# Weighted sums of expert rows in a decoder step: 64x64 tiles of the array in place of 128x128

## The reference

```python
sc, sel = lax.top_k(cand, P_TOPK)
eidx = jnp.take_along_axis(cidx, sel, axis=-1)
g = jax.nn.softmax(sc, axis=-1)
act = jax.nn.gelu(jnp.einsum('td,thkd->thk', xb, u[eidx]))
return jnp.einsum('thk,thkd->td', (g * act), v[eidx])
...
x = x + g2 * peer(n2, ...)
```

## Time and profile before

| | before |
|---|---|
| median of 3 runs | 5520.86 us (5513.3 to 5524.6) |
| the profiled execution | 5515.14 us |
| its span, first to last instruction | 5513.0 us |
| PE busy | 4234.7 us, 77% |
| DVE busy | 2665.5 us, 48% |
| POOL busy | 1701.3 us, 31% |
| ACT busy | 1041.0 us, 19% |
| bytes moved by DMA | 1431.24 MB |

### The profile page before, as it was taken

How to read it: one execution, slowest core, us unless ns; L and a number is a source line. 1 busy time by engine, 2 the same in 40 slices (tenths; PEclk the granted TensorE clock), 3 DMA queues, 4 the chain that set the end, 5 groups by cost and what they waited for, 6 DMA issues and landing times. The chain is left out here.

```text
span 5513.0 us, 49784 instructions
## 1 busy us (share of the span) xinstructions
PE 4234.7 (77%) x14045; PEld 2514.6 (46%) x14045; DVE 2665.5 (48%) x6121; ACT 1041.0 (19%) x2778; POOL 1701.3 (31%) x1436
## 2 busy tenths in 40 slices
PE   6499999999535667939967877778777777777777
PEld 1387766778434563528833333333333333333332
DVE  1201222110346321231157777777776777777775
ACT  0102122110432100010012222222222222222221
POOL 0231221222015300001134444444444444444442
PEclk8699888889757558959878898988889888888888
DMA  6222222122356624131179999999999999999998
GB/s 212 78 82 69 65 77 66 61 75 71 143 200 232 231 97 172 43 100 41 53 290 421 421 421 421 421 421 421 421 421 421 421 421 421 421 421 421 421 421 345
DMA packets 340769, 1431.24 MB, mean 260 GB/s; under 512 B 41214, under 2 KB 105886, under 8 KB 203395
## 3 DMA queue, kind: packets, MB, share of 16 engines
q0 software_dynamic: 165744, 1156.98, 51.3%
q1 hardware_dynamic: 151940, 229.27, 12.3%
q10 hardware_dynamic: 23000, 43.91, 2.1%
HBM read 1345.38 MB, written 91.87 MB: 261 GB/s over the span
## 5 line engine op out<-in xcount | busy, mean ns | idle before, releaser
L1954 PE MATMUL peer_acc<-uv_ring,diag 128*128 128x512 f32 (+1 forms) x4224 | 2002.4, 635 | 629.0 <-ACT diag L1916 624.7
L1776 POOL DMA_INDIRECT uv_ring<-in_peer_uv,idx_all x1056 | 1204.6, 1141 | 1550.3 <-PE peer_acc L1954 1344.7
L1954 PEld LDWEIGHTS peer_acc<-uv_ring,diag 128*128 128x128 f32 (+1 forms) x4224 | 838.0, 202 | 1798.5 <-issue 1629.5
L1845 DVE SCALAR_TENSOR_TENSOR uv_ring<-uv_ring,n_rows 128x1024 f32<-128x1024 f32 x1056 | 1263.6, 1224 | 582.9 <-DMA uv_ring<-in_peer_uv,idx_all 548.0
L1916 ACT ACTIVATE diag<-ident,weight_all 128x128 f32<-128x128 f32 x1024 | 327.3, 390 | 152.4 <-DVE weight_all L1857 144.0
L1912 ACT ACTIVATE gelu_now<-act_now 128x4 f32<-128x4 f32 x264 | 54.2, 205 | 1541.5 <-DVE uv_ring L1845 1533.3
L729 PE MATMUL h_acc<-in_w_lo,n_hi 128*128 128x512 f32 x720 | 317.3, 441 | 0.0
L729 PE MATMUL h_acc<-in_w_hi,n_lo 128*128 128x512 f32 x720 | 308.4, 428 | 0.0
L729 PE MATMUL h_acc<-in_w_hi,n_hi 128*128 128x512 f32 x720 | 304.9, 424 | 0.0
L725 PE MATMUL h_acc<-n_hi,in_w_lo 128*128 128x512 f32 (+1 forms) x672 | 244.1, 363 | 38.1 <-POOLq L449 38.1
L520 ACT COPY h_stage<-h_acc 128x512 f32<-128x512 f32 x174 | 89.5, 519 | 964.0 <-PE h_acc L729 544.2
(11 more groups left out here) (287 smaller groups left out, 5129.6 us busy)
## 6 DMA issues: line engine op xcount, KB each, us to landing
in_w<-in_w_in POOLq DMA_DIRECT2D x68, 512.0 KB
ada_w<-in_w_ada SPq DMA_DIRECT2D x12, 2048.0 KB
q_broadcast<-qk_rows_dram SPq DMA_DIRECT2D x24, 1024.0 KB
h_r<-h_stage SPq DMA_DIRECT2D x80, 256.0 KB
uv_ring<-in_peer_uv,idx_all POOLq DMA_INDIRECT x1056, 26.4
past_keys<-in_cache_kv_g SPq DMA_DIRECT2D x16, 1024.0 KB
h_t<-h_stage SPq DMA_DIRECT2D x56, 256.0 KB
qk_raw<-h_r SPq DMA_DIRECT2D x8, 1536.0 KB, 8.6
```

The lines of the kernel that those rows point to most:

```text
L1776: nc.gpsimd.indirect_dma_start(uv_ring[:, k % SLOTS_UV, :], None, x["peer_uv"][0], bass.IndirectOffsetOnAxis(ap=idx_all[:, g * TOPK + k:g ...
L1845: nc.vector.scalar_tensor_tensor(out=uv_ring[:, k % SLOTS_UV, 0:D], in0=uv_ring[:, k % SLOTS_UV, 0:D], scalar=1.0, in1=n2_rows[:, :], op0= ...
L1954: ins = nc.tensor.matmul(acc[0:w, c, :], diag[:, k % RING, 0:w], uv_ring[:, k % SLOTS_UV, D + c * 512:D + (c + 1) * 512], start=False, sto ...
```

## The change

For the prompt tiles each expert's matmuls are cut into 64x64 tiles of the array. The first 64 tokens (`r` = 0) use array rows 0 to 63, the last 64 (`r` = 1) rows 64 to 127. The columns, and with them the PSUM partitions that get the result, are `(r + k) % 2 * 64`: for even `k` the same half as the rows, for odd `k` the other. Each `r` has PSUM banks of its own, so `peer_acc` grows to [128, 2, 2, 512]. `diag` shrinks to 64 columns; its pattern `halves` is the identity's left half plus its right half. The two partial sums of each token (even and odd experts) are added when the tile ends: ACT copies all four banks to `half_sums`, and PE multiplies with `halves` into `folded` (`add_halves`, four matmuls 128x64), which DVE reads in the residual. The ninth tile keeps its 128x32 matmuls and passes through the same fold. The zero matmuls that open and close a tile become four each. PE's loops over tiles and steps are now Python loops, so its program is straight code.

```diff
-    diag = sb("diag", [P, RING, P])
+    diag = sb("diag", [P, RING, HALF])
+    halves = sb("halves", [P, HALF])
-    acc = psum("peer_acc", [P, 2, 512])
+    acc = psum("peer_acc", [P, 2, 2, 512])
+    folded = psum("peer_folded", [P, 2, 512])
...
+        nc.vector.tensor_tensor(halves[:], ident[:, 0:HALF], ident[:, HALF:P], ALU.add).then_inc(fold_ready, 1)
...
-            dve.wait_ge(sum_copied, t + 1)
-            link(nc.vector.tensor_tensor(moe_sum[0:w, :], moe_sum[0:w, :], gate[0:w, :], ALU.mult))
+            dve.wait_ge(halves_added, t + 1)
+            link(nc.vector.tensor_tensor(moe_sum[0:w, :], folded[0:w].rearrange("p a b -> p (a b)"), gate[0:w, :], ALU.mult))
...
-                act.wait_ge(y_ready, t)
-            nc.scalar.activation(moe_sum[0:w, :], acc[0:w].rearrange("p a b -> p (a b)"), ACT.Copy).then_inc(sum_copied, 1)
+                act.wait_ge(halves_added, t)
+            nc.scalar.activation(half_sums[:], acc[:], ACT.Copy).then_inc(sum_copied, 1)
...
-            with pe.Fori(first, end) as g:
+            for g in range(first, end):
                 for k in range(TOPK):
                     pe.wait_ge(diag_ready, g * TOPK + (k + 1))
                     pe.wait_ge(uv_landed[k % SLOTS_UV], g * 16 + 16)
-                    for c in range(2):
-                        ins = nc.tensor.matmul(acc[0:w, c, :], diag[:, k % RING, 0:w], uv_ring[:, k % SLOTS_UV, D + c * 512:D + (c + 1) * 512],
-                                               start=False, stop=False)
+                    if g < S_FIRST:
+                        for c in range(2):
+                            for r in range(2):
+                                rows, to = slice(r * HALF, r * HALF + HALF), (r + k) % 2 * HALF
+                                ins = nc.tensor.matmul(acc[to:to + HALF, r, c, :], diag[rows, k % RING, :],
+                                                       uv_ring[rows, k % SLOTS_UV, D + c * 512:D + (c + 1) * 512], start=False, stop=False)
...
                     ins.then_inc(v_free, 1)
...
+        def add_halves(t):
+
+            pe.wait_ge(sum_copied, t + 1)
+            pe.wait_ge(fold_ready, 1)
+            if t:
+                pe.wait_ge(y_ready, t)
+            for r in range(2):
+                for c in range(2):
+                    ins = nc.tensor.matmul(folded[r * HALF:(r + 1) * HALF, c, :], halves[:], half_sums[:, r, c, :],
+                                           start=True, stop=True)
+            ins.then_inc(halves_added, 1)
+
+        for t in range(N_TILES):
+            tile(t, t * PH, t * PH + PH if t < N_TILES - 1 else N_STEPS)
+            if t < N_TILES - 1:
+                add_halves(t)
+        add_halves(N_TILES - 1)
```

More of the change, by code:

```diff
@@ L1647, in peer_phase @@
     FOLD = P // S_TOK
+    HALF = P // 2
     S_FIRST = (N_TILES - 1) * PH
@@ L1679, in peer_phase @@
     x1_rows = sb("x1_rows", [P, D])
+    half_sums = sb("half_sums", [P, 2, 2, 512])
     moe_sum = sb("moe_sum", [P, D])
@@ L1701, in peer_phase @@
     sum_copied = sem("sum_copied")
+    halves_added = sem("halves_added")
     n2_loaded = sem("n2_loaded")
@@ L1921, in copy_sum @@
             if not (isinstance(t, int) and t == 0):
-                act.wait_ge(y_ready, t)
-            nc.scalar.activation(moe_sum[0:w, :], acc[0:w].rearrange("p a b -> p (a b)"), ACT.Copy).then_inc(sum_copied, 1)
+                act.wait_ge(halves_added, t)
+            nc.scalar.activation(half_sums[:], acc[:], ACT.Copy).then_inc(sum_copied, 1)
         exps(0)
-        steps(0, PH, ident, True)
+        act.wait_ge(fold_ready, 1)
+        steps(0, PH, halves, True)
         copy_sum(0, P)
         with act.Fori(1, N_TILES - 1) as t:
-            steps(t * PH, t * PH + PH, ident, True)
+            steps(t * PH, t * PH + PH, halves, True)
             copy_sum(t, P)
-        act.wait_ge(fold_ready, 1)
+        act.wait_ge(fold_ready, 2)
         steps(S_FIRST, N_STEPS - 1, fold, True)
@@ L1938, in _, with tile @@
         pe.wait_ge(consts_ready, 3)
[L1940 to L1945, removed]
+        def tile(t, first, end):
+            if t:
                 pe.wait_ge(sum_copied, t)
+            for r in range(2):
                 for c in range(2):
-                    nc.tensor.matmul(acc[:, c, :], zeros[:, 0:P], zeros[:, :], start=True, stop=False)
-            with pe.Fori(first, end) as g:
+                    ins = nc.tensor.matmul(acc[:, r, c, :], zeros[:, 0:P], zeros[:, :], start=True, stop=False)
+            if t == 0:
+                ins.then_inc(v_free, SLOTS_UV)
+            for g in range(first, end):
                 for k in range(TOPK):
@@ L1952, in tile @@
                     pe.wait_ge(uv_landed[k % SLOTS_UV], g * 16 + 16)
-                    for c in range(2):
-                        ins = nc.tensor.matmul(acc[0:w, c, :], diag[:, k % RING, 0:w], uv_ring[:, k % SLOTS_UV, D + c * 512:D + (c + 1) * 512],
-                                               start=False, stop=False)
+                    if g < S_FIRST:
[4 more added lines that the diff above has]
+                                                       uv_ring[rows, k % SLOTS_UV, D + c * 512:D + (c + 1) * 512], start=False, stop=False)
+                    else:
+                        rows = slice(0, P)
+                        for c in range(2):
+                            ins = nc.tensor.matmul(acc[0:S_TOK, 0, c, :], diag[:, k % RING, 0:S_TOK],
+                                                   uv_ring[rows, k % SLOTS_UV, D + c * 512:D + (c + 1) * 512], start=False, stop=False)
@@ L1956, in tile @@
                     ins.then_inc(v_free, 1)
-            for c in range(2):
-                ins = nc.tensor.matmul(acc[:, c, :], zeros[:, 0:P], zeros[:, :], start=False, stop=True)
+            for r in range(2):
+                for c in range(2):
+                    ins = nc.tensor.matmul(acc[:, r, c, :], zeros[:, 0:P], zeros[:, :], start=False, stop=True)
             ins.then_inc(sum_ready, 1)
-        tile(0, 0, PH, P)
-        with pe.Fori(1, N_TILES - 1) as t:
-            tile(t, t * PH, t * PH + PH, P)
@@ L1965, in _ @@
-        tile(N_TILES - 1, S_FIRST, N_STEPS, S_TOK)
+        def add_halves(t):
+            pe.wait_ge(sum_copied, t + 1)
+            pe.wait_ge(fold_ready, 1)
+            if t:
+                pe.wait_ge(y_ready, t)
+            for r in range(2):
+                for c in range(2):
+                    ins = nc.tensor.matmul(folded[r * HALF:(r + 1) * HALF, c, :], halves[:], half_sums[:, r, c, :],
+                                           start=True, stop=True)
+            ins.then_inc(halves_added, 1)
```

## The result

The changed kernel takes **5529.72 us** (median; 5519.7 to 5546.33), the kernel before, run on the same chip in turns with it, 5516.39 us (5513.3 to 5524.6). The ratio is **1.0024, 95% interval 1.0015 to 1.0033**: slower by 0.24%, 13 us. The profiled execution took 5525.42 us with a span of 5523.9 us; of before it was 5515.14 and 5513.0.

What follows compares the result with a forecast made beforehand. Gather DMA was taken to bound the expert stage: 5515.1 + 0 (matmuls) + 0 (boundaries) + 6.1 (tail) + 5.6 (code) = 5526.8 us, or 5532.6 on the median's footing. Forecast 5533 us, range 5517 to 5585.

Steps and rivals of the forecast that it cites:

- What bounds: Expert stage: the DMA queue of expert-row gathers sets the pace, share 1.01 at 421 GB/s, 2.51 us an expert.
- PE's work: Expert matmuls in the stage: 0.86 to 1.71 us an expert, under the DMA's 2.51 us, so worth 0.
- Rival 3: Expert matmuls: tiles run singly, PE needs 3.43 us an expert, stage grows 940 us to about 6465 us; chance 0.05.
- Tile boundaries: The 8 tile ends: PE late by 1 to 8 us, covered by 18 us of queued DMA work, so 0.
- Code: PE's straight code in the expert stage: 71 fetches of 16 KB on the full DMA, +5.6 us.
- even spread: PE's code fetches fall evenly on all 16 DMA engines: 89/16 = 5.6 us; likeliest case, chance 0.50.
- bounds of two engines or one: PE's code fetches in the stage: 45 us if on two DMA engines, 89 us if on one.
- Rival 1: PE's code fetches fall on few DMA engines: 5572 us on two, 5616 us on one; chance 0.28.
- Rival 2: Expert stage: code fetches stay hidden and only the tail counts, 5527 us, within 0.2%; chance 0.10.
- Tail: After the last expert: more zero records, a larger copy and the fold, without cover, +6.1 us (5 to 10).
- Gathers take longer from issue to landing: Sign in the expert stage: gathers' time from issue to landing rises from 26.3 us.
- POOL waiting less for PE: Sign in the expert stage: POOL, which issues the gathers, waits less for PE; no size given.

Runs made afterwards that it cites:

- e1: The changed kernel with PE's tiles and steps back in loops on the chip, as in the kernel before; ratio to before 1.0004.
- e9: The changed kernel with PE in loops, only u halves gathered, and even and odd experts kept to the columns of their own row half; 4762.51 us.
- e8: The changed kernel with PE in loops, gathering only the u half of each row, dots over 512 columns; 4566.88 us.
- e3: The changed kernel with 17 more instructions on PE for each prompt expert, waits that are always met; ratio to before 1.0049.
- e10: The kernel before with POOL's gathers in a loop over pairs of steps instead of straight code; ratio to before 0.9995.
- e12: The kernel before with more always-met waits on POOL ahead of every gather, thus more POOL code to fetch; ratio to before 1.0084.
- e7: The changed kernel, PE's code straight, gathering only the u half of each row, dots over 512 columns; 4561.86 us.
- e2: The kernel before with PE's loops written out as straight code, nothing else changed; ratio to before 1.0002.
- e11: The changed kernel with POOL's gathers in a loop over pairs of steps, PE's code still straight; ratio to before 1.0028.
- half-row kernels: The kernel before and the changed kernel, each gathering only the u half of each row, dots over 512 columns; 4730.06 and 4561.86 us.

## Why the prediction was right, and where its terms were not

The forecast was 5533 us, 0.21% over before, and the result is 0.24% over (1.0015 to 1.0033). Its mechanism holds: matmuls worth nothing, code and tail the whole cost. The sum was 11.7 us and the two traces differ in stage and tail by 12.0; but two terms missed in opposite directions, the code by 3.4 us and the tail by 3.1. That the total is so close is luck.

- **What bounds.** Right: DMA share 1.01 and 421 GB/s on both sides, steps of 40.17 us.
- **PE's work, 0 in the stage.** Right, by e1's stage (0.1 us). The range of 0.86 to 1.71 us for an expert was right: 3.89 us for four is 0.97 us each with the first one's filling in it. Rival 3 (singly running tiles) is out. Tiles in different rows and columns run together here, by the 3.89 us against 7.15 us, and e9 against e8 shows the condition: four do not when consecutive experts stay in the same column halves (1.83 us an expert against 1.62, with PE busy for 396 of 400 us against 326).
- **Tile boundaries, 0.** Right, by e1 again. At the boundary of the earlier trace rows the order of things was as foreseen, with the end of the residual, the fold, the zeros and POOL's gather:

```profile
4124.09 1.22 DVE L1883 TENSOR_TENSOR x_rows<-x_rows,moe_sum 128x1024 f32<-128x1024 f32 x1
...
4125.46 2.85 PE L1985 MATMUL peer_folded<-half_sums,halves 128*64 128x512 f32 x8 [3.58 <-DVE x_rows L1883]
4128.24 4.44 PE L1953 MATMUL peer_acc<-zeros 128*128 128x512 f32 x8
...
4132.61 2.86 PE L1964 MATMUL peer_acc<-uv_ring,diag 64*64 64x512 f32 x24
...
4135.33 0.94 POOL L1781 DMA_INDIRECT uv_ring<-in_peer_uv,idx_all  x1 [13.73 <-PE peer_acc L1964]
```

  From the end of the residual (4125.31 us) PE takes 7.3 us to the first expert, where before took 5.9: 1.4 us more, at the low end of the 1 to 8 foreseen. POOL's gather comes 10.0 us after the residual, where before had 10.4 (4120.83 to 4131.27), so it is not late at all. The 4 us between 4131.27 and 4135.33 lie ahead of this boundary: the residual itself ends 4.5 us later, by the time the stage had lost so far.
- **Code, +5.6 foreseen, +9.0 measured.** This term was mis-sized, and its mechanism was half right. The right half: the fetches take time of the DMA engines that the gathers fill (0.2% of the 16 engines' time for the 67 on queue 8 in after's table, and 22.5 us more of stage for 137 fetches in e3), and the last of 16 parts sets a gather's landing. The number of fetches was right (71 foreseen, 69 more measured). The step that failed is the even spread: I had the fetch near 3170 us, which delayed nothing, and read it as spreading over all 16 engines. It said only that the part it moved was not the latest one. Eight parts are late in after, not 16, and a fetch puts one back by 1.5 us, not 1.26. That makes 69 x 1.5 / 8 = 12.9 us, less the lead that POOL's late part gave to all others (2.7 us by e10, 3.3 by the landings): about 10 us for 9.0 measured. The packet of a fetch itself takes 1.07 us in after's records (median of 67) and one of POOL's 0.31 us; why they put one part back by 1.5 and 0.70 us is not shown. The bounds of two engines or one were too far out for PE. Rival 1's reason for them, that a processor's fetches always go to one engine, fits POOL's (in e12 one part is 15.3 us late, and 67 fetches cost 46.6 us) and not PE's (eight parts late).
- **Rival 2, the code hidden.** Out: the stage grew by 9.0 us for 69 fetches and by 22.5 for 137. Where the DMA has room nothing contradicts it, but e8 against e7 could not show 9 us.
- **Tail, +6.1 foreseen, +3.0 in this pair.** The four zeros came out right (1.93 to 3.65 us, +1.7) and so did the copy (1.02 to 1.89 us, +0.9 for 0.7). The fold took 1.98 us, under the range of 2.6 to 7 and under the 3.4 us of eight records in a row, so some of them overlap; presumably that is because its halves, too, go to different column halves. And the 16 records of the sample tile, which the change does not touch, took 7.05 us after and 8.66 before, because the granted clock was 1.00 in the one and 0.81 in the other. In e2, e10 and e12, whose tails are before's, they take 7.05 us and the tail 17.9 us; so at the same clock the tail grew by 22.5 - 17.9 = 4.6 us, 1.5 under the forecast, and the fold is the term that was too large. In e11, at a granted clock of 0.70, they take 10.01 us, the fold 3.15 at 0.56, and the tail 26.7.
- **Gathers take longer from issue to landing.** The row says the opposite: a median of 21.6 us after, 26.3 before. But that view takes its median from few gathers: 61 of before, all of slot 8 of the ring, and 123 of after, of slots 0 and 9, and the time to landing depends on the slot (19.5 us for slot 0 and 30.2 for slot 15 in before). Over all gathers of the stretch whose 16 records of completion are in the trace (868 and 966) the median goes from 25.9 to 27.4 us. Pairing the n-th issue with the n-th dot (gathers 100 to 950) gives a mean of 29.4 us after and 28.5 before. So it came true, and is small.
- The rest of what I said would show it held: PE's busy time is down by a third, and queue 8 has about 70 fetches. **POOL waiting less for PE** did not come true. From 2900 to 5400 us it waits as long as before. The waits (engine, line, waited for: us in total, times, longest) are, in after and then in before:

```profile
POOL uv_ring L1781 <- PE peer_acc L1964: 1275.3, 302, 16.8
```

```profile
POOL uv_ring L1776 <- PE peer_acc L1954: 1274.4, 720, 14.7
```

  The likely reason, which no run takes apart: POOL issues at the pace at which rows land, and what it does not spend on issuing it spends waiting for a slot, however fast PE gives one back. It waits less often (302 times for 720) and longer.

Stage and tail together account for the ratios, if before's tail is taken as 17.9 us: after's 9.0 + 4.6 is 0.25% for a measured 0.24; e11's 1.2 + 9.0 + (26.7 - 17.9) is 19.0 us, 0.34% for a measured 0.28 (0.17 to 0.38); e3's 22.5 + 4.6 is 0.49% for 0.49; e12's 46.6 is 0.84% for 0.84.

## What to carry to other kernels

When a stage runs with its DMA engines full, ask of an edit not what it does for the compute engines but what it adds to the DMA, instruction code included: loops written out on PE cost 9 us here, while the matmuls, almost twice as fast, gave nothing. Ask then on which of the 16 engines the addition falls, since the last of a gather's 16 parts ends the wait for it: half a megabyte that held back one part alone cost 47 us here. The alternating 64x64 form itself is worth taking wherever PE is the bound (168 us in the half-row kernels), with its steps kept in a loop if the DMA is full.

## What the runs showed of the hardware beyond what I had expected

- PE's code fetches, 16 KB each, hold back eight of a gather's 16 parts, one after another (1.5 us of one part for each): all eight are late by 12.0 to 14.4 us at the end of after's stage. POOL's, 8 KB each, all hold back one and the same (0.70 us each in e12, where it ends 15.3 us late; 0.6 to 0.7 us for three of before's).
- A DMA share of 1.01 at 421 GB/s does not say that a gather's 16 parts keep level: before had one part 3.3 us behind all others, and after has eight some 12 us or more behind the first, with 421 GB/s in both. In e12, with one part 15 us behind, the share is still 1.01 (3000 to 5400 us) and only the GB/s fall, to 415.
- 64x64 float32 matmuls fill four tiles here (0.97 us an expert at a granted clock of 1.00) when consecutive experts alternate between column halves, and two when they don't: 1.62 against 1.83 us an expert in e8 and e9.
- A gathered row of half the length takes 57% of the DMA's time for a whole one (159 against 280 ns a packet, e7 and before), not 50%.
